# Where the last projection is summed: later latent halves of `w_out` in the scores' banks, norm sums and residual copies moved

## What is computed

```python
x, ctx = fnet_layer(x, ctx)             # mixer, then swiglu with ffn_w_in[0], ffn_w_out[0]
x = diff_attention_layer(x, ctx)        # attention, then swiglu with ffn_w_in[1], ffn_w_out[1]
h_res = concatenate([meta, x])          # 16 + 256 tokens
proj = rmsnorm(h_res) @ w_in            # q_lat, kv_lat, k_pe, g_mla, na_q, na_k, na_v, g_na
y_mla = mla(rmsnorm(q_lat) @ w_uq, rmsnorm(kv_lat) @ w_ukv, ...) * silu(g_mla)   # 1024 wide
y_na = neighbourhood_attention(na_q, na_k, na_v) * silu(g_na)                    # 1024 wide
out = (h_res + concatenate([y_mla, y_na]) @ w_out)[16:]                          # w_out: 2048 x 1024
```

## Time and profile before

| | |
|---|---|
| median of 3 runs | 1244.82 us (1242.17 to 1246.73) |
| the profiled execution | its time 1238.1 us, its span 1236.4 us |
| PE, busy | 1177.6 us, 95% of the span |
| VectorE | 709.3 us, 57% |
| ScalarE | 540.4 us, 44% |
| GpSimd | 88.7 us, 7% |
| mean granted clock of PE | 0.992 of full |

### The profile page before, as it was taken

One profiled execution on the slowest core, in us unless ns is written; L12 is line 12 of the kernel. 1 busy time (PEld: TensorE's weight loads), 2 busy tenths in 40 slices (PEclk: granted clock), 3 DMA queues, 4 the chain that ended last, 5 costly groups with the idle time before them and its releaser, 6 DMA issues.

```text
span 1236.4 us, 18606 instructions
## 1 busy us (share of the span) xinstructions
PE 1177.6 (95%) x7072; PEld 981.7 (79%) x7072; DVE 709.3 (57%) x1193; ACT 540.4 (44%) x1000; POOL 88.7 (7%) x133
## 2 busy tenths in 40 slices
PE   7999999999999999799999989999988999999988
PEld 4666787787788888578975889999978986799656
DVE  4544667767723334777679654445566565445764
ACT  3243422222222323544458654444446566466652
POOL 0002011122100000200000100000000000210500
PEclk9999999999999999999999989999999999999999
DMA  9889456578722322123420345555535442254220
GB/s 315 317 278 328 139 172 199 176 247 284 248 69 103 103 91 82 42 91 103 134 71 1 101 140 183 190 173 176 170 103 161 129 126 88 74 173 167 72 69 34
DMA packets 121671, 183.02 MB, mean 148 GB/s; under 512 B 4498, under 2 KB 92897, under 8 KB 121601
## 3 DMA queue, kind: packets, MB, share of 16 engines
q1 hardware_dynamic: 113888, 154.64, 37.6%
q0 software_dynamic: 7712, 27.43, 6.8%
HBM read 180.68 MB, written 1.05 MB: 147 GB/s over the span
## 4 chain that ended last, share of the span: by engine, by line
PE 82%; DVE 9%; ACT 5%; issue 3%; POOL 1%; DMA 0%; DVEq 0%; SPq 0%; ACTq 0%; POOLq 0%
PE ps L489 20%; PE ps L490 20%; PE ps L491 20%; PE ps L822 2%; PE ps L823 2%; PE ps L824 2%; PE ps L863 2%; ACT wh L467 2%; PE ps L2212 1%; PE ps L2256 1%; DVE hl L622 1%; DVE nrm L606 1%; DVE wl L474 1%; DVE nm L1135 1%; POOL big L644 1%
## 5 line engine op out<-in xcount | busy, mean ns | idle before, releaser
L489 PE MATMUL ps<-hh,wh 128*128 128x256 f32 (+2 forms) x1272 | 426.2, 335 | 18.0 <-DVE hl L622 9.9
L474 DVE TENSOR_TENSOR wl<-raw,wh 128x1024 fp32r<-128x1024 f32 (+1 forms) x246 | 295.7, 1208 | 248.8 <-ACT wh L467 245.5
L490 PE MATMUL ps<-hl,wh 128*128 128x256 f32 (+2 forms) x1272 | 416.2, 327 | 0.0
L491 PE MATMUL ps<-hh,wl 128*128 128x256 f32 (+2 forms) x1272 | 415.4, 327 | 0.0
L467 ACT ACTIVATE wh<-raw 128x1024 fp32r<-128x1024 f32 (+1 forms) x246 | 252.5, 1032 | 277.3 <-PE ps L491 262.4
L489 PEld LDWEIGHTS ps<-hh,wh 128*128 128x128 f32 x1272 | 242.2, 190 | 60.3 <-issue 27.3
L490 PEld LDWEIGHTS ps<-hl,wh 128*128 128x128 f32 x1272 | 241.4, 190 | 22.5 <-issue 1.9
L491 PEld LDWEIGHTS ps<-hh,wl 128*128 128x128 f32 x1272 | 242.3, 190 | 21.0
L489 PE MATMUL ps<-ah,wh 128*128 128x256 f32 (+2 forms) x376 | 126.6, 337 | 1.1 <-DVE big L2026 0.8
L490 PE MATMUL ps<-al,wh 128*128 128x256 f32 (+2 forms) x376 | 124.4, 331 | 0.0
L491 PE MATMUL ps<-ah,wl 128*128 128x256 f32 (+2 forms) x376 | 124.3, 331 | 0.0
(11 more groups left out here) (241 smaller groups left out, 1441.1 us busy)
## 6 DMA issues: line engine op xcount, KB each, us to landing
raw<-in_ffn_w_in SPq DMA_DIRECT2D x44, 1024.0 KB, 5.2
raw<-in_ffn_w_out SPq DMA_DIRECT2D x22, 1024.0 KB, 4.9
raw<-in_w_in SPq DMA_DIRECT2D x22, 1024.0 KB, 5.4
big<-in_w_ada SPq DMA_DIRECT2D x16, 1024.0 KB, 9.5
big<-in_w_ada POOLq DMA_DIRECT2D x24, 512.0 KB, 4.4
ex<-in_w_ada POOLq DMA_DIRECT2D x24, 512.0 KB, 5.3
raw<-in_diff_w_in SPq DMA_DIRECT2D x12, 1024.0 KB, 5.1
raw<-in_w_out SPq DMA_DIRECT2D x8, 1024.0 KB, 4.9
```

The costliest lines, as they stand in the source:

```text
L474: ins = nc.vector.tensor_tensor(place(wl), v, place(wh).bitcast(F32), ALU.subtract)
L489: nc.tensor.matmul(o, w_hi, m_hi, start=first, stop=False, **kw)
L490: nc.tensor.matmul(o, w_hi, m_lo, start=False, stop=False, **kw)
L491: return nc.tensor.matmul(o, w_lo, m_hi, start=False, stop=last, **kw)
```

## The change

- *Norm sums:* all four norms now send 6 tiles through GpSimd (`N_ADDED`). For "ffn1" and "second" that is two more GpSimd adds and two fewer sums on PE.
- *Residual copies:* VectorE copies banks 6 and 7 (second token tile) ahead of `LAT_UNITS`; ScalarE copies banks 4 and 5 (first tile) between the norm "lat" and the gate units. The sums of "lat" move to banks 7 and 6, so PE waits for VectorE's copies (`s_xtv`) ahead of them; it waits for ScalarE's (`s_xta`) ahead of `MLA_UNITS`. The gate units use banks 0, 1 and 2.
- *Halves 0 to 3 of the last projection:* `latent_part` takes one half of one quarter at a time (three matmuls), one on even and two on odd steps from 4 to 14.
- *Halves 4 to 7:* no longer in bank 7 and `x_tok`. `out_half` sums them in banks 0 to 3, half 4 in step 17 (once the last scores' maximum is taken), 5 in step 18, 6 in step 19, then 7 to 15. VectorE's four additions of these groups are gone.

```diff
-        GATHERED = {"ffn0": KD - 2, "diff": KD - 2, "ffn1": KD - 4, "second": KD - 4}
+        GATHERED = ["ffn0", "diff", "ffn1", "second"]
+        N_ADDED = KD - 2
...
-                "second": [(0, 0, L2)], "lat": [(2, 0, L), (3, L, HW)]}
+                "second": [(0, 0, L2)], "lat": [(7, 0, L), (6, L, HW)]}
...
-            banks = (0, 1, 2, 5, 6, 7) if phase is MLA_UNITS else (0, 1) if phase is GATE_UNITS else (0, 1, 2)
+            banks = (0, 1, 2, 5, 6, 7) if phase is MLA_UNITS else (0, 1, 2)
...
-        PART_AT = {}
-        for x in range(8):
-            PART_AT.setdefault(5 + x, []).append(divmod(x, 2))
-        PART_AT.update({17: [(4, 0)], 18: [(4, 1)], 19: [(5, 0), (5, 1)]})
-        PARTS_IN = 6
+        PART_AT, parts = {}, [(g, k) for g in range(4) for k in range(4)]
+        for i in range(4, 15):
+            n = 1 + i % 2
+            PART_AT[i], parts = parts[:n], parts[n:]
...
+        def latent_part(pe, g, k):
+
+            t, c = divmod(g, 2)
+            if g and k == 0:
+                pe.wait_ge(s_part, g)
+            q = OUT_Q + k
+            if g == 0:
+                pe.wait_ge(split, q + 1)
...
+            nc.tensor.matmul(ps[:, 7, :], a_h, w_h, start=(k == 0), stop=False)
+            nc.tensor.matmul(ps[:, 7, :], a_h, w_l, start=False, stop=False)
+            ins = nc.tensor.matmul(ps[:, 7, :], a_l, w_h, start=False, stop=(k == 3))
+            if g == 3:
+                ins.then_inc(used, 1)
+            elif k == 3:
                 ins.then_inc(s_fill, 1)
...
-                for g in range(PARTS_IN):
-                    if (g, 1) in PART_AT.get(i - 1, ()):
+                for g in range(4):
+                    if (g, 3) in PART_AT.get(i - 1, ()):
                         latent_added(dve, g)
...
+            act.wait_ge(s_xt, 1)
+            act.wait_ge(s_h, BASE["second"] + KD)
+            for c in range(2):
+                ins = nc.scalar.activation(x_tok[:, 0, c * 512:(c + 1) * 512], ps[:, 4 + c, :], ACT.Copy)
+            ins.then_inc(s_xta, 1)
...
+            dve.wait_ge(s_xt, 1)
+            dve.wait_ge(s_h, BASE["second"] + KD)
+            for c in range(2):
+                ins = nc.vector.tensor_copy(x_tok[:, 1, c * 512:(c + 1) * 512], ps[:, 6 + c, :])
+            ins.then_inc(s_xtv, 1)
             link(nc.vector.memset(mv[0:32 + N_META, 2, :], 0.0))
             units_dve(dve, link, mark, LAT_UNITS)
             norm_dve(dve, "lat")
-            units_dve(dve, link, mark, GATE_UNITS[:3])
-            dve.wait_ge(s_xt, 1)
-            dve.wait_ge(s_h, BASE["second"] + KD)
-            for c in range(4):
-                ins = nc.vector.tensor_copy(x_tok[:, c // 2, c % 2 * 512:(c % 2 + 1) * 512], ps[:, 4 + c, :])
-                if c == 1:
-                    units_dve(dve, link, mark, GATE_UNITS[3:5])
-            ins.then_inc(s_xtv, 1)
-            units_dve(dve, link, mark, GATE_UNITS[5:])
+            units_dve(dve, link, mark, GATE_UNITS)
...
             na_dve(dve, link, mark)
-            latent_added(dve, 6)
-            split_next(dve, OUT_Q + 4)
-            latent_added(dve, 7)
-            split_next(dve, OUT_Q + 5, 7)
-            dve.wait_ge(s_part, 8)
+            split_next(dve, OUT_Q + 4, 8)
+            dve.wait_ge(s_part, 4)
...
+            pe.wait_ge(s_xtv, 1)
             norm_pe(pe, "lat")
             units_pe(pe, GATE_UNITS, before=1)
             pe.wait_ge(s_h, BASE["lat"] + 2)
-            pe.wait_ge(s_xtv, 1)
+            pe.wait_ge(s_xta, 1)
...
-                pe.wait_ge(s_os, NA_G0 + k - 8 + 1)
+                if k >= 8:
+                    pe.wait_ge(s_os, NA_G0 + k - 8 + 1)
                 for t in range(2):
-                    at = t * P
-                    a_h, a_l = hh[:, k - 8, at:at + P], hl[:, k - 8, at:at + P]
+                    at = (L2 + t * P) if k < 8 else t * P
+                    a_h, a_l = hh[:, k % 8, at:at + P], hl[:, k % 8, at:at + P]
...
-            na_pe(pe, lambda i: None)
-            for g in range(PARTS_IN, 8):
-                for half in range(2):
-                    latent_part(pe, g, half)
-            for k in range(8, 16):
+            def na_tail(i):
+
+                if i > NA_STEPS:
+                    if i == NA_STEPS + 1:
+                        pe.wait_ge(s_mx, na_max_done(NA_STEPS - 1))
+                    out_half(i - NA_STEPS + 3)
+
+            na_pe(pe, na_tail)
+            for k in range(7, 16):
                 out_half(k)
```

More of the change, by code:

```diff
@@ L414, in build @@
         s_xt = sem("x_turned_by_tokens")
+        s_xta = sem("x_turned_out_act")
         s_xtv = sem("x_turned_out_dve")
@@ L535, in build @@
         SUMS = {"ffn0": [(5, 0, NT)], "diff": [(0, 0, NT)], "ffn1": [(7, 0, L)],
-                "second": [(0, 0, L2)], "lat": [(2, 0, L), (3, L, HW)]}
-        GATHERED = {"ffn0": KD - 2, "diff": KD - 2, "ffn1": KD - 4, "second": KD - 4}
+                "second": [(0, 0, L2)], "lat": [(7, 0, L), (6, L, HW)]}
+        GATHERED = ["ffn0", "diff", "ffn1", "second"]
+        N_ADDED = KD - 2
         sq_acc = big[:, 13312:13824]
         def added_before(name, k):
[L543 to L547, removed]
+            return GATHERED.index(name) * (N_ADDED - 1) + max(k, 0)
         def norm_square(act, name, k):
@@ L554, in norm_square @@
                 act.wait_ge(s_x, X_OF[name] + k + 1)
-            if k >= 2 and name in GATHERED and k - 2 < GATHERED[name]:
+            if name in GATHERED and k >= 2:
                 act.wait_ge(s_added, added_before(name, max(k - 2, 1)))
@@ L636, in squares_added @@
             n = sum(p[2] for p in NORMS[name][2])
-            for k in range(1, GATHERED[name]):
+            for k in range(1, N_ADDED):
                 pool.wait_ge(s_sq, BASE[name] + k + 1)
@@ L648, in norm_sum @@
             tiles, _, parts, _, _ = NORMS[name]
-            if name in GATHERED and k < GATHERED[name]:
-                if k == GATHERED[name] - 1:
+            if name in GATHERED and k < N_ADDED:
+                if k == N_ADDED - 1:
                     pe.wait_ge(s_added, added_before(name, k))
@@ L653, in norm_sum @@
                     nc.tensor.matmul(ps[:, bank, 0:b - a], T["ones"], sq_acc[:, a:b], start=True, stop=False)\
-                        .then_inc(s_sum, GATHERED[name])
+                        .then_inc(s_sum, N_ADDED)
                 return
@@ L1270, in build @@
         OUT_Q = 2 * G["out2"]
-        PART_AT = {}
-        for x in range(8):
-            PART_AT.setdefault(5 + x, []).append(divmod(x, 2))
-        PART_AT.update({17: [(4, 0)], 18: [(4, 1)], 19: [(5, 0), (5, 1)]})
-        PARTS_IN = 6
+        PART_AT, parts = {}, [(g, k) for g in range(4) for k in range(4)]
+        for i in range(4, 15):
+            n = 1 + i % 2
+            PART_AT[i], parts = parts[:n], parts[n:]
+        assert not parts
         ROUND_AT = {2: [-2], 3: [-1], 13: [0], 14: [1], 15: [2], 16: [3]}
[L1278 to L1282, removed]
+        def latent_part(pe, g, k):
+            t, c = divmod(g, 2)
+            if g and k == 0:
@@ L1283, in latent_part @@
                 pe.wait_ge(s_part, g)
[L1284 to L1296, removed]
@@ L1297, in latent_part @@
-            if half and b < 3:
+            q = OUT_Q + k
+            if g == 0:
+                pe.wait_ge(split, q + 1)
+            n = slice(c * 512, (c + 1) * 512)
+            at = L2 + t * P
+            w_h, w_l = wh[:, q % SPLIT_SLOTS, n], wl[:, q % SPLIT_SLOTS, n]
+            a_h, a_l = hh[:, k, at:at + P], hl[:, k, at:at + P]
+            nc.tensor.matmul(ps[:, 7, :], a_h, w_h, start=(k == 0), stop=False)
+            nc.tensor.matmul(ps[:, 7, :], a_h, w_l, start=False, stop=False)
@@ L1309, in latent_added @@
-            tile = x_tok[:, b // 2, b % 2 * 512:(b % 2 + 1) * 512]
+            if g == 3:
+                dve.wait_ge(used, OUT_Q + 4)
+            else:
+                dve.wait_ge(s_fill, g + 1)
+            tile = x_tok[:, g // 2, g % 2 * 512:(g % 2 + 1) * 512]
             nc.vector.tensor_tensor(tile, ps[:, 7, :], tile, ALU.add).then_inc(s_part, 1)
@@ L1357, in na_pe @@
                     ins.then_inc(s_pv, 1)
-                for g, half in PART_AT.get(i, ()):
-                    latent_part(pe, g, half)
+                for g, k in PART_AT.get(i, ()):
+                    latent_part(pe, g, k)
                 tail(i)
@@ L2542, in out_half @@
                         w_h, w_l = wh[:, q % SPLIT_SLOTS, n], wl[:, q % SPLIT_SLOTS, n]
-                        nc.tensor.matmul(o, a_h, w_h, start=(k == 8), stop=False, skip_group_check=True)
+                        nc.tensor.matmul(o, a_h, w_h, start=(k == 4), stop=False, skip_group_check=True)
                         nc.tensor.matmul(o, a_h, w_l, start=False, stop=False, skip_group_check=True)
```

7 lines of the change are left out of this document (removed).

## The result

The changed kernel took 1232.06 us in the median of five runs (1229.77 to 1232.71), the kernel before 1242.17 in five runs beside it (1240.16 to 1246.73). The ratio is 0.9908, 95% interval 0.9886 to 0.9931: faster by 0.7 to 1.1%. Run again later, six runs of it gave 1231.71 (1230.43 to 1233.55), ratio 0.9919 (0.9901 to 0.9937). I forecast 1236.4, in a range of 1232 to 1242. The sign was right; the gain, some 10 to 11 us in the medians, was larger than my 8.4, and puts the time at the lower edge of the range (1232.06) or just outside it (1231.71).

What follows compares the result with a forecast made beforehand. PE, busy 95% of the span, was taken as the bound, so only its idle time counted. Terms -0.85 - 2.8 + 1.3 - 2.05 + 0.7 - 4.75 gave -8.45 us, from 1244.8 to 1236.4; range 1232 to 1242, eight in ten.

Steps and rivals of the forecast that it cites:

- ffn1 norm: Norm sums before the ffn1 stage: five PE sums become three, GpSimd's two added adds are covered, -0.85 us.
- Second norm: Norm before the second block: ScalarE's round starts at 913.35 instead of 916.21 and all that follows moves along, -2.8 us.
- rival C: Waits in the norm, before the last latent unit and before gate 4 each bring 1.2 GHz: -3.9, 1240.9 us; chance 0.16.
- GpSimd's adds: Second norm: each add takes 0.77 us, against 1.36 beside VectorE's splits, with 0.1 us between them.
- Rival B: GpSimd's adds in the second norm take 1.36 us beside VectorE's x updates: -5.6, 1239.2 us; chance 0.12.
- Residual copies: Two VectorE copies ahead of the latent units, in a queue without a gap to hide them: +1.3 us.
- Third gate bank: Gate units: unit 4 waits instead of unit 3, with 1.5 us of wait left, -2.05 us.
- Spread: First four halves of the last projection, in the attention steps: a 1.5 us wait in step 9, +0.7 us in all.
- Last projection: Later halves straight into banks 0 to 3: the end takes 34.6 instead of 39.35 us, -4.75 us.
- Rival E: Attention stretch falls to 1.2 GHz and the output halves start in it: slower, 1258 us with eight halves; chance 0.04.
- rival D: Step 9's wait is swallowed, the end starts on time and the norm gives 3: -9.7, 1235 us; chance 0.08.

Runs made afterwards that it cites:

- E12: The changed kernel with one latent part moved from step 9 to 10 and all four residual copies on VectorE, between and behind the last latent splits: 1226.69 us.
- E7: The changed kernel with one latent part moved from step 9 to 10 and VectorE's two residual copies and memset behind the latent units: 1228.78 us.
- E4: The changed kernel with the first four halves in eight visits of six matmuls, as in the kernel before: 1231.26 us.
- E11: The changed kernel with two banks for the gate units instead of three: 1237.96 us.
- E6: The changed kernel with the residual copies and two gate banks of the kernel before: 1233.78 us.
- E8: The changed kernel with eight of the sixteen x_lat transposes moved into PE's wait for GpSimd's adds in the second norm: 1232.23 us.
- E10: The changed kernel with the last projection and its spread as in the kernel before: 1235.19 us.

## Why the prediction was right in its sign and wrong in its time

By the steps of the prediction:

- **ffn1 norm**, forecast -0.85: -0.9. Right, and GpSimd's two added adds were covered.
- **Second norm**, forecast -2.8: -1.2 in the profiles, -2.6 where the clock stayed up. The chain of GpSimd and the 2.3 us wait were right; the step that failed is the one from "the round starts then" to "all that follows moves with it". What follows waits for PE's sums: `rstd` stands behind the round for 0.23 us more at 2.4 GHz and for 1.65 us more at 1.2 (the two rows for L569 above). I had named the second case as "about 1 us more" and as the lower bound, and taken the upper end. In eight of the fourteen profiles the clock fell in this place: in all four with the old sums and a wait of 1.9 us, and in four of the ten with the new. This is the one of rival C's three falls that came.
- **GpSimd's adds**: right, 0.77 forecast, 0.76 measured, with the 0.1 between them. The row of 3.48 us above is four adds with their gaps; the groups of instructions have the adds alone (total, mean ns):

```profile
L642 POOL TENSOR_TENSOR big<-big,sq 128x272 f32<-128x272 f32 x4 | 3.0, 762 | 1.1 <-ACT sq L559 0.7
```

  They ran beside VectorE's updates of x, which read PSUM and SBUF, as fast as in the kernel before, while one add of the ffn1 norm took 1.36 us beside splits. Rival B is out. The rule of the Trainium skill weighed above (GPSIMD Engine Reference, 8. Key points), contention with VectorE's two-SBUF-input instructions, agrees with this.
- **Residual copies**, +1.3: +1.2. Right in size and in place, a queue without a gap; the delay shows as the new wait of 0.9 for the key unit's norm, and the split's wait stayed at 1.2. E12 shows the cost was one of position: between and behind the last splits the same copies, and two more, bring no wait of PE.
- **Third gate bank**: the wait left was 1.3 us (forecast 1.5), and no profile with three banks shows 1.2 GHz behind it. Rival C's other two falls did not come, and the term was right, but **the sum was not**. I wrote of the -2.05 "All with the +1.3 in it" and then added the +1.3 again. The gate stage gave 3.4, the copies took 1.2, net 2.2. Added up rightly my terms are -9.75.
- **Spread**, +0.7: +0.75, with the wait of 1.4 us in step 9 as worked out. E7 removes it by moving one part. E4 shows that the old spread is worth as much as the new one, within the noise: what the one loses in step 9 the other loses in waits at the end of the stretch.
- **Last projection**, -4.75: -4.85, 34.5 us against 34.6 forecast, no wait for the added partial sums (before's L1310) or for a split. Rival E, 1258 us, is out; stretches at 1.2 GHz of 3 to 7 us in the attention exist in other profiles, with the old spread too.

So between the profiles the sum was right by two errors of opposite sign: 1.3 counted twice, and 1.6 too much hope for the norm. That it met the profile to 0.15 us was luck. The line on the bounds was added up wrong as well: as they stand the bounds of the terms give -11.0 to -1.3, not "-14 to +0.1"; and rival D, -8.45 with 0.7 and 0.2 more, comes to -9.35 and not to -9.7.

**The time.** The step that failed is the last line of the sum: "The median of the runs is 6.7 us above that time, and 1244.8 - 8.4 is 1236.4." It takes the distance from the profiled execution to the median for a constant of the kernel. It is none. Before's executions range from 1237.4 to 1247.3 us with the share of time at 1.2 GHz, and its profile was one of the fastest; the changed kernel's lie within 4 us, and their median 2 us, not 6.7, above its profile. From 1236.4 to the measured 1231.7 it goes like this: 2.3 us because three runs had put before's median at 1244.8 where 57 put it at 1242.5; 1.3 for the double counting; -1.6 for the norm; the rest is 2.7. The clock accounts for it: the two profiles differ by 0.002 of clock, the averages of the runs by 0.0051, and 0.0031 more at 0.9 us for 0.001 is 2.8 us. This is an estimate, from clocks that are given to 0.001.

Is the clock's share caused by the edits? It is best supported at the gates: E11, one line of code, brings back a wait of 4.1 us and with it the stretch at 1.2 GHz and 0.003 of mean clock, while E6's profile has a wait of 3.2 us there and no such stretch. For the kernel as a whole it is supported less: one part alone raised the mean clock from 0.9876 to 0.989, all three to 0.9927, pairs lie at 0.991 and 0.993. It isn't a sum over the parts. Why executions of one program differ in where the clock falls, as at 701 or 912 us in the two profiles of the changed kernel, stays open; no run here controls it.

## What to carry to other kernels

Price a change against several executions, or read the granted clock of the one profile first and ask where in the spread of the runs it lies. A removed wait of TensorE can be worth more than its length, since the work behind it may have run at 1.2 GHz; but moving TensorE work into one wait out of another gained nothing (E8). Small copies on a full queue cost their length and in a gap of the same queue nothing, so look where the engine waits for its own input (E12, with one partial sum moved too: 5 us below the changed kernel with the same work in another order and two copies on another engine). And where a term is worked out net of another, write that beside it in the sum.

## What the runs showed that I had not expected

- Where TensorE's clock falls differs between executions of one program: the same 2.32 us wait was followed by three sums in 3.0 us (913 us at 0.50) in one and in 1.6 us in the other.
- The times of before lie in groups that follow the mean granted clock: about 1238 us at 0.992, 1242 at 0.987, 1245 at 0.984, the slope being 0.9 us for each 0.001.
- Whether the clock fell in the second norm went with what it had done 200 us before: with a stretch at 1.2 GHz near 702 us it never did (five profiles), without one it did in eight of nine.
- The later adds' three waits, 2.3 us in all, cost their length but, with the other parts in, no clock: E10 had 0.9932.
